# Last chunks' decays two chunks ahead, attention's scale in the queries' norm, and x loaded and transposed ahead of the second modulation tile

## Time and profile before

| | us |
|---|---|
| median of 3 runs | 1221.64 |
| lowest and highest | 1221.28, 1224.31 |
| the profiled execution | 1221.2 |
| its span, first to last instruction | 1219.4 |
| PE busy | 1146.8 |
| DVE busy | 643.8 |
| ACT busy | 338.6 |
| POOL busy | 112.9 |
| mean granted TensorE clock | 0.960 |

### The profile page before, as it was taken

The page is one execution under the profiler, slowest core; times in us unless marked ns, Lnnn a source line. Parts: engine busy times, 40 slices in busy tenths (PEclk is TensorE's granted clock), DMA queues, the critical chain, the costliest instruction groups (busy, mean ns, idle before and its releaser), DMA issues.

```text
span 1219.4 us, 15604 instructions
## 1 busy us (share of the span) xinstructions
PE 1146.8 (94%) x6191; PEld 798.5 (65%) x6191; DVE 643.8 (53%) x1366; ACT 338.6 (28%) x788; POOL 112.9 (9%) x107
## 2 busy tenths in 40 slices
PE   4899999989868898999999999999999999999998
PEld 2545857657768587546558888744556478888543
DVE  2222125757876855599615566650598326656400
ACT  2212223765453231523311212200525121121100
POOL 0000101200120011054000000010162000000000
PEclk9899989989788987999999999999999999999999
DMA  9723232000003202353237445423532254444410
GB/s 357 258 77 110 92 124 74 1 1 1 2 1 94 91 20 69 138 207 131 77 90 230 138 150 177 157 104 103 207 136 72 69 189 156 139 138 163 177 40 35
DMA packets 96666, 140.06 MB, mean 115 GB/s; under 512 B 12207, under 2 KB 63058, under 8 KB 96466
## 3 DMA queue, kind: packets, MB, share of 16 engines
q1 hardware_dynamic: 95684, 136.84, 33.0%
q10 hardware_dynamic: 910, 2.22, 0.5%
HBM read 138.01 MB, written 1.05 MB: 114 GB/s over the span
## 4 chain that ended last, share of the span: by engine, by line
PE 76%; DVE 17%; ACT 3%; issue 2%; DMA 1%; SPq 0%; POOL 0%; DVEq 0%; ACTq 0%
PE bank L1330 25%; PE bank L1349 12%; PE bank L815 12%; PE bank L480 2%; PE bank L473 2%; PE bank L1158 2%; DVE work L2584 1%; PE bank L620 1%; DMA ring<-in_ada_w 1%; PE bank L1092 1%; PE bank L1148 1%; DVE work L2579 1%; PE bank L1033 1%; PE bank L599 1%; PE bank L649 1%
## 5 line engine op out<-in xcount | busy, mean ns | idle before, releaser
L1330 PE MATMUL bank<-work,ring 128*128 128x256 f32 x1024 | 222.7, 379 | 0.0
L1330 PEld LDWEIGHTS bank<-work,ring 128*128 128x128 f32 x1024 | 194.2, 190 | 26.2
L815 PE MATMUL bank<-work,ring 128*128 128x256 f32 (+1 forms) x432 | 142.9, 490 | 2.3 <-ACT work L1402 2.3
L1349 PE MATMUL bank<-ring,work 128*128 128x512 f32 x288 | 124.3, 592 | 0.0
L815 PEld LDWEIGHTS bank<-work,ring 128*128 128x128 f32 x432 | 83.7, 197 | 56.9 <-issue 47.6
L1853 ACT ACTIVATE work<-work,prm 128x256 f32<-128x256 f32 x88 | 48.0, 593 | 250.5 <-DVE work L2724 224.0
L1349 PEld LDWEIGHTS bank<-ring,work 128*128 128x128 f32 x288 | 54.7, 190 | 68.0 <-issue 67.4
L2716 DVE TENSOR_TENSOR work<-bank,turned 128x512 f32<-128x512 f32 x44 | 30.4, 691 | 112.0 <-PE bank L1330 112.0
L1330 PE MATMUL bank<-work 128*128 128x256 f32 x384 | 83.9, 379 | 0.0
L1330 PEld LDWEIGHTS bank<-work 128*128 128x128 f32 x384 | 73.0, 190 | 9.9
L2734 DVE SCALAR_TENSOR_TENSOR work<-work,prm 128x256 f32<-128x256 f32 x176 | 77.1, 479 | 4.2 <-ACT work L1853 2.6
(11 more groups left out here) (454 smaller groups left out, 1758.3 us busy)
## 6 DMA issues: line engine op xcount, KB each, us to landing
ring<-in_w_up SPq DMA_DIRECT2D x32, 1024.0 KB, 7.7
ring<-in_w_in SPq DMA_DIRECT2D x24, 1024.0 KB, 7.6
ring<-in_w_down SPq DMA_DIRECT2D x16, 1024.0 KB, 6.0
ring<-in_ada_w SPq DMA_DIRECT2D x12, 1024.0 KB, 11.5
work<-in_w_up SPq DMA_DIRECT2D x12, 1024.0 KB, 7.8
ring<-in_w_out SPq DMA_DIRECT2D x10, 1024.0 KB, 7.0
work<-in_w_in SPq DMA_DIRECT2D x4, 1024.0 KB, 8.4
work<-in_w_down SPq DMA_DIRECT2D x4, 1024.0 KB, 6.0
```

The source lines that it names most:

```text
L815: ins = mm(b[0:rows, 0:toks], wt[:, k, off:off + rows], hT[:, k, 0:toks], start=(k == 0), stop=(k == KD - 1))
L1330: ins = mm(b[:, SEQ * half:SEQ * half + SEQ], wt[:, KD * half + k, P * j:P * j + P], xnT[:, k, :], start=(k == 0), stop=(k == KD - 1))
L1349: ins = mm(acc[2 * t + j][:, :], actT[:, k, P * t:P * t + P], wt[:, q, 512 * j:512 * j + 512], start=(k == 0), stop=(k == FB - 1))
```

## The change

There are four edits.

1. PE and ACT make the decays of step n + 2 in iteration n (n = 4, 5), where they made those of step n + 1. On PE they stand behind `reads(n)` and ahead of `keyed_values(n)`; on ACT the tanh rows and key rates stand behind `take_products(n)` and ahead of `take_keyed_values(n)`. Those of step 5 stay ahead of everything. DVE's order stays as it was.
2. The attention's scale is no longer applied to the scores: the variance of the queries' norm is multiplied by scale to the power -2, so its inverse root carries the scale. The exponential has no scale, and the row maximum goes straight into the bias: the 16 small multiplications L2004 on DVE are gone.
3. x and ctx are loaded by SP, ahead of `ada` 0, where ACT's queue loaded them.
4. PE transposes x and ctx behind `modulation_rows(0)`, ahead of `modulation_rows(1)`; the columns of row 0 come behind row 1. ACT squares x ahead of taking row 0, and copies `hT` ahead of taking row 1.

```diff
@@ PE, start
             modulation_rows(0)
-            modulation_rows(1)
-            modulation_columns("mod", mod_rows, 0, range(4))
-
             pe.wait_ge(S["xs"], 4)
             for k in range(KD):
...
                 ins.then_inc(*filling(("hT", k)))
+            modulation_rows(1)
+            modulation_columns("mod", mod_rows, 0, range(4))
             modulation_rows(2)
@@ PE, last chunks
             for n in range(4, 8):
                 keys, tokens, reads = prepare(n)
-                if n < 7:
-                    decays_and_rates(n + 1)
+                if n == 4:
+                    decays_and_rates(5)
                 keys()
...
                 tokens()
                 reads()
+                if n < 6:
+                    decays_and_rates(n + 2)
                 keyed_values(n)
@@ ACT, start
-            for j, name in enumerate(("x", "ctx")):
-                act.dma_start(xc[:, 2 * j:2 * j + 2, :], w[name].rearrange("a (t p) d -> p (a t) d", p=P)).then_inc(S["x_in"], 16)
...
-            take_row(0)
             act.wait_ge(S["x_in"], 32)
...
-            take_row(1)
+            take_row(0)
             for k in range(0, KD, 2):
...
+            take_row(1)
             take_row(2)
@@ ACT, attention
-                    A.activation(prob[:, q, :], b[:, :], ACT.Exp, bias=small[:, 167 + q:168 + q], scale=ATTN_SCALE,
+                    A.activation(prob[:, q, :], b[:, :], ACT.Exp, bias=small[:, 167 + q:168 + q],
@@ ACT, last chunks
+            tanh_rows(5)
+            key_rates(5)
             for n in range(4, 8):
-                if n < 7:
-                    tanh_rows(n + 1)
-                    key_rates(n + 1)
                 take_blocks(n)
...
                 take_products(n)
+                if n < 6:
+                    tanh_rows(n + 2)
+                    key_rates(n + 2)
                 take_keyed_values(n)
@@ DVE
-                V.tensor_reduce(small[:, 164 + q:165 + q], b[:, :], AX_X, MAX, negate=True).then_inc(S["vec_step"], 1)
-                vec.wait_ge(S["vec_step"], next(vec_steps))
-                TS(small[:, 167 + q:168 + q], small[:, 164 + q:165 + q], ATTN_SCALE, None, MUL).then_inc(S["m_bias"], 1)
+                V.tensor_reduce(small[:, 167 + q:168 + q], b[:, :], AX_X, MAX, negate=True).then_inc(S["m_bias"], 1)
...
-            TS(small[:, 120:122], b[:, 0:2], 1.0 / Q_LORA, EPS, MUL, ADD).then_inc(S["vec_step"], 1)
+            TS(small[:, 120:122], b[:, 0:2], ATTN_SCALE ** -2 / Q_LORA, ATTN_SCALE ** -2 * EPS, MUL, ADD).then_inc(S["vec_step"], 1)
@@ SP, ahead of the tiles
+            for j, name in enumerate(("x", "ctx")):
+                sp.dma_start(xc[:, 2 * j:2 * j + 2, :], w[name].rearrange("a (t p) d -> p (a t) d", p=P)).then_inc(S["x_in"], 16)
```

## The result

| | before | after |
|---|---|---|
| median, us | 1221.66 (20 runs, 1215.54 to 1228.15) | 1214.05 (20 runs, 1211.56 to 1218.69) |
| the profiled execution, us | 1221.2 | 1215.5 |
| its span, us | 1219.4 | 1213.7 |
| PE busy, us | 1146.8 | 1145.4 |
| DVE busy, us | 643.8 | 641.5 |

The ratio is 0.9936, with a 95% interval of 0.9918 to 0.9954: 7.6 us faster, where 1214.7 was forecast and 1214.05 came. The 20 runs of before spread over 12 us, six of them above 1226, and those of after over 7, so one execution alone says little of a change of 6 us. Each stretch has to be read for itself. The stretches explain the 5.7 us between the two profiled executions and not all of the 7.6 between the medians, since no execution above 1226 was profiled.

The account below looks back on a forecast made before the run. PE was taken to hold 76% of the chain of waits, DVE 17%. Start 0.2, attention 0.8 and last chunks 5.5 sum to 6.5 us off 1221.2, giving 1214.7 us, range 1208.5 to 1218.5.

Parts of the forecast that it names:

- the second gap: Last chunks: PE's wait for DVE's masks ahead of step 5's reads, expected to shrink from 3.88 us to 1.8.
- The third gap: Last chunks: PE's 3.27 us wait for DVE's mask before step 6's second reads, expected not to shrink, half clock returning behind.
- The start, -0.2: Before the first projection: edits 3 and 4 start it at 37.25 us instead of 37.48; bounds -3 to +3 us.
- The tie: Start: the first projection needs modulated `hT`, ready at 37.34 us, and weight tile `in` 0, landed at 37.2.
- Attention, -0.8: Attention: dropped multiplications save DVE 0.4 us, an earlier exponential 0.19 us at first and last maximum; bounds 0 to -2.4.
- The last chunks, -2.8 and -1.1: Last chunks: DVE's waits for ACT's tanh rows vanish, saving 2.8 us in step 6 and 1.06 us in step 7.
- the floor: Last chunks: 3.9 us gained from DVE's two vanished waits for ACT alone, without any clock gain.
- The clock, -1.6: Last chunks: step 5's reads keep full clock behind the smaller gap, so DVE's masks follow PE by 1.6 us less.
- (a): Last chunks: both gaps still cost the clock, giving 3.9 us there, 4.9 in all, 1216.3 us; chance 0.22.
- (b): Last chunks: clock returns behind the third gap or doesn't fall, 10.5 to 11.5 us there, 1209.5 us; chance 0.17.
- (c): Last chunks: a bank or copy holds PE instead, only 0 to 2.8 us won, 1218 to 1220.5 us; chance 0.12.
- (d): Last chunks: half clock lasts into the solves, some 10 us of matmuls doubling, 1224.7 us or more; chance 0.05.

Follow-up runs that it names:

- the decays alone: Kernel before with edit 1 alone, decays of steps 6 and 7 two chunks ahead on PE and ACT: median 1214.58 us, ratio 0.9921.
- the scale alone: Kernel before with edit 2 alone, no multiplication behind the 16 row maxima: median 1221.44 us, ratio 0.998.
- before with extra matmuls: Kernel before plus four 128x512 matmuls, results unused, in PE's gap of 3.27 us, nothing of the change: median 1214.42 us, ratio 0.9915.
- masks and extra matmuls together: Changed kernel with DVE's masks ahead of its key rates in steps 5 and 6, plus four unused matmuls in PE's gap: median 1212.07 us, ratio 0.9895.

## Why the prediction was right, point by point

The total (1214.7 forecast, 1214.05 measured) and its main mechanism hold: DVE's waits for ACT are gone, the second gap shrank and kept the clock. That the total fits to 0.7 us is in part luck. The third gap grew and the clock gave more, which cancelled; and the measured 7.6 us holds a part that no profile explains, since edits 2 to 4 were to give 1.0 and measured 5.4 (3.1 to 7.6).

- **The start, -0.2.** Every time of it was met in the profiled execution, 37.05 for 37.25, and that was luck. Of eight profiles with edits 3 and 4 one has the projection between 37.0 and 37.5; the others have it at 38.22 to 40.26, 38.9 on average with the first. Of four without these edits (before, the decays alone, the scale alone, and before with extra matmuls) two have it at 37.5 and two at 40.0 and 40.35, 38.8 on average. The tie that was worked out isn't what held the projection in the seven: rows 3 at low clock made `hT` late, and ACT's last step released it. The bound of 3 us either way, for a clock kept or lost, was the right size; with 0.9983 (0.9961 to 1.0006) for both edits alone, no gain is shown.
- **Attention, -0.8.** It measured -1.0, as idle time of PE, in every profile. The step that was off is the 0.08 us of DVE for each multiplication: it is 0.19. From the last maximum that waits for PE to the last of all, DVE needs 14.14 us before (292.57 to 306.71) and 13.21 after (294.44 to 307.65), 0.93 less for five of them, where 0.4 was taken. The whole of that does not reach PE: with 0.19 the prediction's sum would be 1.3, and 1.0 came. 0.19 of it is at the first maximum, as said, and 0.8 around the last two. That the 0.19 is the reduce's signal and DVE's wait for it, beside the instruction itself, is likely but was not tried apart. The 16 instructions are 2.4 us of DVE's busy time.
- **The last chunks, -2.8 and -1.1.** Both waits of DVE went, as said, and "the masks come at 342.2": they came at 340.77, since the scan began at 335.31 and not 336.35, and they were 5.46 us behind it where 5.88 was taken. The second gap, 1.54 us, is inside the 1.5 to 2.2 that the prediction named.
- **The third gap** is the step that failed. "The third gap does not shrink" is right, but 2.4 to 3.7 us was named and it grew to 4.79. The 3.9 us of the floor were counted as won in full, and 1.5 of them came back here: over the profiles with and without edit 1, PE's idle time from decays to solves is 11.3 and 13.8 us on average (3 and 6 profiles), 2.4 less, not 3.9. DVE needs 6.43 us from its scan (350.36) to its masks (356.79) (L2037 takes 0.57 us in this place, for one). PE was done with its earlier work at 351.67 + 1.16 = 352.8, where before it was at 360.6 by this row of the kernel before:

```profile
359.39 1.16 PE L620 MATMUL bank<-work 64*128 64x128 f32 x16 [1.32 <-ACT work L1489]
```

That is 7.7 us earlier, to masks that came only 6.2 us earlier (357.62 for 363.83). Of the 7.7, 1.32 is a wait for ACT's `take_blocks(6)`, which stood behind the tanh rows; it went with them, and the prediction hadn't counted it.
- **The clock, -1.6.** It gave more: busy time 54.7 us on average with edit 1 and 58.0 without, 3.3 less. The reads of step 5 at 1.00 in place of 0.51 were named. Waits and clock together are 5.7 us, beside the 5.5 forecast; the sum was right with a split that was not. The split is rougher than the sum: idle time is 10.8 to 11.8 us with edit 1 and 12.6 to 14.9 without, and goes down where busy time goes up, while the lengths of the two groups lie 4 us apart.
- **Rivals.** (a), that the smaller gap still costs the clock, falls: 341.60 to 348.50 is at 1.00. (b) falls in this kernel: the clock is 0.50 from 358.00 to 366.00 with PE busy all of it, as in the earlier trace rows. The rule of the Trainium skill that activity releases the clock ("TensorE: Matmul & The Clock Gate", Part 1) is not borne out by these 8 us; by 371.50 the clock is back. What (b) would be worth was shown by filling the gap: 6.4 us of the stretch by the profile beside it, 4.3 by the first, where 5 to 6 had been worked out. (c) falls, since the waits of L2030 are gone and the solves come 6.8 us earlier. By the prediction's own terms it would have been 1217.4 to 1220.2, where 1218 to 1220.5 is written. (d) did not occur: the low clock ended before the solves.

What stays open is why one gap costs the clock and another does not. Gaps of 0.60, 1.07 and 1.54 us kept it in these profiles, of 2.66, 3.27, 3.88 and 4.79 lost it; but at the start 1.56 us kept it once and lost it three times in the same instructions, and 1.64 lost it with masks and extra matmuls together. So the length of one gap is not all of it.

## What to carry to other kernels

Where PE waits for another engine, read what the clock does behind the wait before you price the wait: here taking 4 us of idle time away gave no gain that could be told, and four matmuls that compute nothing, in a bank that was free anyway, were worth 6.8 us. Split every stretch into PE's idle and busy time: the idle time repeats to 0.02 us where a wait is fixed, while the busy time carries the clock's scatter, and so a gain of 1 us can be shown in a kernel whose runs spread over 12. Where the waits follow PE's own pace, as in the last chunks, the two trade against each other, and the length of the stretch over several profiles is the firmer number. Take more than one profile before you call a time met: one of eight starts was where the prediction had it. When a wait is moved away, follow the waiting engine to its next meeting: PE came 7.7 us earlier to masks that DVE brought only 6.2 us earlier.

## What the runs showed of the hardware that was not expected

- Removing a 128x1 multiplication and the semaphore wait in front of it shortened DVE's path by 0.19 us, more than the 0.15 us that the instruction's own row shows.
- PE stays at 0.50 over 8 us of uninterrupted matmuls behind a gap, and at 1.00 over the same matmuls when the gap holds other ones.
- Eight float32 matmuls of 128x512 take 7.13 us (16 records, 0.45 us each), four take 3.70.
- The same program on the same data started its first projection at 37.05 and at 39.16 us: a load landed 1.1 us later, and 16 matmuls behind it took 3.32 us in place of 1.92.
